# Gate and up chunks of the FFN: 16 products with the high weights, then 16 with the low weights

## What is computed

```python
def swiglu(h, w_in, w_out):
    a, b = jnp.split(h @ w_in, 2, axis=-1)
    return (jax.nn.silu(a) * b) @ w_out

def swiglu_2(x, wg, wu, wd):
    return (jax.nn.silu(x @ wg) * (x @ wu)) @ wd
```

## Time and profile before

| | us |
|---|---|
| median of the runs | 2282.01 |
| the runs | 2281.63, 3823.35, 2282.01 |
| span of the profiled execution | 2277.3 |
| difference of median and span (what lies around the span) | 4.7 |

### The profile page before, as it was taken

How to read it: one execution, slowest core, us unless ns; L and a number is a source line. 1 busy time by engine, 2 the same in 40 slices (tenths; PEclk the granted TensorE clock), 3 DMA queues, 4 the chain that set the end, 5 groups by cost and what they waited for, 6 DMA issues and landing times.

```text
span 2277.3 us, 32617 instructions
## 1 busy us (share of the span) xinstructions
PE 2193.1 (96%) x13722; PEld 1878.6 (82%) x13722; DVE 1360.6 (60%) x1568; ACT 957.9 (42%) x1078; POOL 124.5 (5%) x69
## 2 busy tenths in 40 slices
PE   6999999999999998999999999999999999999999
PEld 4887788888888767888888898888988897878888
DVE  4358834756755364565666674657656677536665
ACT  3312424445544243444444362444444466234443
POOL 0066500000000000000000000000000011000000
PEclk9999999999999999999999999999999999999999
DMA  8328904554555312455555333554455442124552
GB/s 327 111 93 333 408 18 153 185 184 166 185 184 185 138 37 74 178 192 184 186 186 192 137 139 130 187 189 177 167 184 187 164 152 108 40 84 149 187 192 81
DMA packets 52529, 373.10 MB, mean 164 GB/s; under 512 B 5776, under 2 KB 6800, under 8 KB 7888
## 3 DMA queue, kind: packets, MB, share of 16 engines
q1 hardware_dynamic: 51632, 367.78, 44.2%
q0 software_dynamic: 800, 3.93, 0.5%
HBM read 370.64 MB, written 1.05 MB: 163 GB/s over the span
## 4 chain that ended last, share of the span: by engine, by line
PE 89%; DVE 6%; ACT 2%; DMA 2%; issue 1%; POOL 0%; SPq 0%; ACTq 0%; DVEq 0%; POOLq 0%
PE PS L360 23%; PE PS L361 12%; PE PS L375 6%; PE PS L377 6%; PE PS L376 6%; PE PS L312 5%; PE PS L647 4%; PE PS L1345 2%; PE PS L294 2%; PE PS L195 2%; PE PS L295 2%; PE PS L296 2%; PE PS L800 2%; DMA ring<-stream 1%; PE PS L277 1%; PE PS L278 1%
## 5 line engine op out<-in xcount | busy, mean ns | idle before, releaser
L360 PE MATMUL PS<-AR_r 128*128 128x512 f32 x2240 | 792.9, 398 | 0.0
L480 DVE TENSOR_TENSOR ring_r<-ring,AR_r 128x2048 fp32r<-128x2048 f32 x270 | 619.3, 2299 | 289.0 <-ACT AR_r L474 288.9
L474 ACT ACTIVATE AR_r<-ring 128x2048 fp32r<-128x2048 f32 x274 | 522.4, 1911 | 315.1 <-PE PS L377 194.0
L361 PE MATMUL PS<-AR_r,ring_r 128*128 128x256 f32 x2240 | 628.2, 280 | 0.0
L360 PEld LDWEIGHTS PS<-AR_r 128*128 128x128 f32 x2240 | 420.8, 188 | 103.1
L361 PEld LDWEIGHTS PS<-AR_r,ring_r 128*128 128x128 f32 x2240 | 422.8, 189 | 2.5
L532 ACT ACTIVATE AR<-PS 128x512 f32<-128x512 f32 x140 | 83.7, 598 | 439.7 <-PE PS L361 439.7
L375 PE MATMUL PS<-AR_r 128*128 128x512 f32 x616 | 242.1, 393 | 0.0
L377 PE MATMUL PS<-AR_r 128*128 128x512 f32 x616 | 240.8, 391 | 0.0
L376 PE MATMUL PS<-ring_r,AR_r 128*128 128x512 f32 x616 | 240.1, 390 | 0.0
L594 DVE TENSOR_TENSOR AR<-AR,PS 128x512 f32<-128x512 f32 x70 | 48.1, 687 | 151.6 <-ACT AR L532 151.6
(11 more groups left out here) (386 smaller groups left out, 3042.3 us busy)
## 6 DMA issues: line engine op xcount, KB each, us to landing
ring<-stream SPq DMA_DIRECT2D x346, 1024.0 KB, 4.8
X<-xt SPq DMA_DIRECT2D x1, 2048.0 KB, 10.3
AR<-bias POOLq DMA_DIRECT2D x1, 1536.0 KB, 6.9
AR<-pt POOLq DMA_DIRECT2D x2, 512.0 KB, 3.7
out<-X SPq DMA_DIRECT2D x4, 256.0 KB, 2.1
SM<-small SPq DMA_DIRECT2D x1, 545.0 KB, 4.3
AR<-invc SPq DMA_DIRECT2D x1, 512.0 KB, 15.3
X<-negl POOLq DMA_DIRECT2D x1, 512.0 KB, 6.2
```

Source lines behind the costliest of these rows:

```text
L360: pe.matmul(PS[:, bank, :], w_hi, X_PARTS[:, :, k * T:(k + 1) * T], start=(k == 0), stop=False, skip_group_check=True)
L361: ins = pe.matmul(PS[:, bank, 0:T], w_lo, X_HI[:, k, :], start=False, stop=(k == DT - 1), skip_group_check=True)
L474: act.activation(w_hi_of(tag, i), ring[:, n % SLOTS, :], ACT.Identity).then_inc(split_hi, 1)
L480: dve.tensor_tensor(RING_R[:, n % SLOTS, :], ring[:, n % SLOTS, :], w_hi_of(tag, i), ALU.subtract).then_inc(split_lo, 1)
```

## The change

In `gate_up` the inner loop is cut in two. A chunk now begins with a wait on `split_hi` in place of `split_lo`, goes through all 16 products with the high weights (both banks), then waits on `split_lo`, and goes through the 16 products with the low weights. The products, their operands, their PSUM targets, the number of weight loads, the wait for the banks and the `multiplied` signal at the end are the same.

```diff
                 for half in range(2):
                     n = n0 + i + half
-                    need_split(r, i + half)
+                    pe.wait_ge(split_hi, r + (s0 + i + half + 1))
...
                         for k in range(DT):
                             w = slice(k * 256 + j * P, k * 256 + (j + 1) * P)
-                            w_hi, w_lo = w_hi_of(tag, i + half)[:, w], RING_R[:, n % SLOTS, w]
-                            pe.matmul(PS[:, bank, :], w_hi, X_PARTS[:, :, k * T:(k + 1) * T], start=(k == 0), stop=False, skip_group_check=True)
-                            ins = pe.matmul(PS[:, bank, 0:T], w_lo, X_HI[:, k, :], start=False, stop=(k == DT - 1), skip_group_check=True)
+                            pe.matmul(PS[:, bank, :], w_hi_of(tag, i + half)[:, w], X_PARTS[:, :, k * T:(k + 1) * T], start=(k == 0), stop=False, skip_group_check=True)
+                    need_split(r, i + half)
+                    for j in range(2):
+                        bank = (6, 4)[half] + j
+                        for k in range(DT):
+                            w = slice(k * 256 + j * P, k * 256 + (j + 1) * P)
+                            ins = pe.matmul(PS[:, bank, 0:T], RING_R[:, n % SLOTS, w], X_HI[:, k, :], start=False, stop=(k == DT - 1), skip_group_check=True)
                     ins.then_inc(multiplied, 1)
```

## The result

| | before | changed |
|---|---|---|
| median, first timing, us | 2282.24 | 2263.03 |
| ratio, 95% interval | | 0.9926 (0.9913 to 0.9939) |
| median, timed again (e8), us | 2279.07 | 2264.95 |
| ratio, 95% interval | | 0.9936 (0.9921 to 0.9950) |
| span of the profiled execution, us | 2277.3 | 2259.1 |

The kernel got faster by 0.6 to 0.7%, 14.6 us by the longer timing (0.0064 x 2279; interval 11.4 to 18.0). One of the four runs of before, 3823.35 us, was in a slow state and does not count in the ratios. The two medians of the first timing alone lie 19.2 us apart (2263.03 / 2282.24 = 0.9916), but before has only three runs there, all near 2282; in the later timings it had medians of 2279.07 to 2280.24. I had said 8, and a range that ended at 2268. The direction was right, the size was not.

The account below looks back on a forecast made before the run. TensorE, which never waits, was taken to be bound by its own pace; later blocks -8.2, six first blocks +0.4, one -0.1 sum to -7.9 us, so 2282.0 to 2274.1; its own range 2269 to 2279, overall range 2268 to 2286.

Parts of the forecast that it names:

- The waits: At chunk head and mid-chunk in gate_up: TensorE arrives 5.4 us or more after the later signal, so worth 0.
- The order: In gate_up, 16 x 512-wide then 16 x 256-wide instead of alternating: all that is left, -7.9 us in sum.
- The price of the two homogeneous halves: In a gate_up chunk: 0.2267 us per 512-wide and 0.1200 per 256-wide product, together 11.09 us per block.
- A: Rival: the slow pace belongs to the gate_up stage, not the alternation; block stays 11.29, time 2282; chance 0.22.
- B: Rival: the 512-wide product with two-piece operand is itself slow, 0.235 us each; time 2288.0; chance 0.12.
- C: Rival: the mid-chunk wait breaks the lead of weight loads, 11.6 us on top of the forecast, 2285.8; chance 0.05.
- a transient that alternating products leave behind: Surplus of a `down` chunk behind a gate_up block, 0.07 us; added once per block, at the up chunk's high half.
- the `down` chunks stand behind 256-wide products as before: Claim that the change leaves `down` chunks as they were: 0 us.
- later block: A gate_up block not first of its FFN: 11.29 to 11.16 us, -0.13 x 63 = -8.2 us.
- My lower bound: No transient at all in gate_up: blocks 11.09 against 11.29, together -12.9 us, time 2269.1.
- what lies around the span: Profiled span 2277.3 lies 4.7 us under the median 2282.0; the forecast median kept that distance.
- The page against the rows: In the low half, each weight load, about 107 ns by the skill, has just one 107 ns product to hide under.

Follow-up runs that it names:

- e8: The changed kernel itself once more, timed more often, against the kernel before: 2264.95 us, ratio 0.9936.
- e1: Kernel before, alternating order kept, with only the changed kernel's two waits (split_hi at the head, split_lo before the first low product): ratio 1.0005.
- e2: Changed kernel's order, 16 high then 16 low products, behind the single wait on split_lo at the chunk's head: ratio 0.9936 against before.
- e6: Kernel before, alternating, the 512-wide product reading its operand in one piece instead of two: later blocks 11.29 and 11.30 us, time not read.
- e7: Kernel before, alternating, with the low product 512 wide too: 64 products in 14.51 us, 0.2267 each, time not read.
- e5: Kernel before with four extra transposes in front of each gate chunk: 2302.6 us; later blocks 11.38 or 11.39 (28) and 11.17 or 11.18 (35).
- e4: Per bank 2 high products, then 2 low ones, in turn, one wait per chunk: ratio 0.9945 against before, blocks 11.13 and 11.14 us.
- e3: Per bank 8 high products, then 8 low ones, one wait per chunk: ratio 0.9946 against before, blocks 11.14 and 11.15 us.
- e9: Changed kernel with both high halves (gate, up) first, then both low halves, each behind its own wait: ratio 0.9942 against before.

## Why the prediction was wrong

**Right.** The waits are worth 0 (e1) and the wait in mid-chunk costs 0 (e2). The order is what gains, as the prediction said. The price of the two homogeneous halves was right: 0.2267 for a 512-wide product (16 of them in 3.63) and 0.1200 for a 256-wide one (16 in 1.91 to 1.92; the first, behind a wide one, takes 0.114, the others 0.120). Each rival fell: A, that the slow pace belongs to the stage, by the blocks themselves; B by e6; C by e2.

**The term that failed.** I read the 0.07 us by which one `down` chunk exceeds the next as "a transient that alternating products leave behind", and then charged it to a passage that has no alternation before it: once to the up chunk. And I left `down` at 5.50, since "the `down` chunks stand behind 256-wide products as before". That is true of the last product alone. What stood ahead was the slow alternation, now it is a run of narrow products, and that passage costs less than half: `down` takes 5.46 or 5.47 against 5.44 in e7, 0.02 to 0.03 us more, the same as in the up chunk (3.65 against 3.63). The rows of before already had the smaller price: behind the fast block of the earlier trace rows the `down` chunk takes 1131.70 - 1126.23 = 5.47, not 5.51. So the change took the larger part of the surplus out of the `down` chunks behind slow blocks too, a term that I had put at nothing. By the steps of the sum:

| | forecast | measured |
|---|---|---|
| later block | 11.29 to 11.16 | 11.29 to 11.105 |
| all 70 blocks | -7.9 us | -11.4 us |
| 77 `down` chunks | 0 | -2.3 us |
| sum | -7.9 us | -13.7 us |

These 5.8 us are the part of the miss that the profiles show in the changed stages. The forecast of 2274.1 missed the first timing's 2263.03 by 11.1; the other 5.3 us are not in these stages.

**The range.** My lower bound took the passage at zero in the blocks, -12.9 us, and held `down` fixed even there, though the row that I used for the transient was a `down` chunk. A bound must move every term in which the unknown stands. With `down` at 5.44 behind each of the 70 blocks it would have been 70 x 0.06 = 4.2 us lower, at 2264.9, and the range would just have held the longer timing's 2264.95 but not the first one's 2263.03. The rest is scatter between executions of one kernel, and much of it goes with the clock: beside e5 to e8 before took 2274.7 to 2283.1 us, three executions with a mean granted clock of 0.984 took 2281.5 to 2283.1, two with 0.989 took 2274.7 and 2275.5. I had also read the single profile's 4.7 us of "what lies around the span" as a constant. In each of the four runs of the changed kernel time and span are only 1.8 apart (2260.88 and 2259.1 for one), so some 3 us of the 4.7 was one execution against another.

**What the order really removes.** A step of `gate_up` and `down`, against 11.09 + 5.44 = 16.53 for the plain sum of its products:

| widths change every | step, us | surplus, us |
|---|---|---|
| 1 product (before, slow kind) | 16.79 | 0.26 |
| 2 (e4) | 16.59 | 0.06 |
| 8 (e3) | 16.61 | 0.08 |
| 16 (changed) | 16.57 | 0.04 |
| 32 (e9) | 16.55 | 0.02 |

Most of the gain comes from leaving strict alternation, which runs 6 ns a pair over the sum when it starts as the slow kind; from the longest step here to the shortest (e3 to e9) lie 0.06 us, under 4 us in the whole execution, or 0.2%.

**The page against the rows, once more.** Products of one width stand 227 ns apart at 512 columns and 120 at 256, so 13 ns above their columns at 2.4 GHz. The Trainium skill, "TensorE: Matmul & The Clock Gate", section "Back-to-back issue gap", gives columns plus 2.5 ns for an isolated product, and about 131 ns a product at 512 columns for a stream of weight loads and products. Neither is the pace of this stream; the measured 227 ns decides. The Trainium skill, same page, section "LDWEIGHTS (loading the stationary operand)", gives a load a time of its columns over 1.2, which for 128 columns makes an estimate of 107 ns. The rows agree in so far as 16 narrow products in a row, each with its own load, keep 120 ns, which leaves room for such a load; no run here shows the time of a load by itself (the profile's records of loads are 188 to 192 ns long and overlap).

## What to carry to other kernels

When TensorE never waits, read its pace from the starts, class by class, and compare with the pace of unmixed streams of the same shapes: here 2048 of 2240 pairs stood 6 ns above the sum of their two products, and a reordering without a saved instruction took 0.6% off. In this kernel grouping the products of equal width brought it, and runs of two already gave most of it. And when a price is taken from one row, move that same row with it in the bounds.

## What the runs showed of the hardware that was not expected

- Strictly alternating 512-wide and 256-wide products, each with its own weight load, have two paces, 0.3468 and 0.3532 us a pair, at a granted clock of 1.00. A block keeps the one with which it starts. Behind four or five transposes it is either (35 fast and 28 slow, 34 and 29, of the later blocks); behind `down` and small products of zeros it is always slow (63 of 63), behind other products and the same zeros mostly fast (5 of 7). What sets it stays open.
- The two paces are two patterns. In before, the distances from start to start repeat every three pairs in a slow block (241, 120, 236, 113, 233, 117 ns) and every two in a fast one (233, 117, 231, 112 ns). Of the 31 pairs behind the first, 10 have the 240 ns distance in each of the 64 slow blocks and none in the six fast blocks. What the `down` chunk behind a slow block costs goes with the place where the pattern stops: 5.50 where its first distance is the 241 of the pattern (before), 5.47 in the 28 later slow blocks of e5, where it is 233.
- A run of 512-wide products behind a run of 8 or more 256-wide ones takes 0.02 to 0.04 us more than 0.2267 each (e3, e8), behind other 512-wide ones nothing more (e7).
- Identical stretches far from the change differ by 3.5 us between executions (121.2 and 117.7) with the granted clock at 0.96 or at 1.00: as much as a quarter of the effect studied.
